# The narrow column tile of an expert moved from last to first place, in a two-layer hybrid backbone kernel on one core

## The chip, the core and the metric

The kernel runs on one core of a Trainium2 chip. The metric is the device time of one execution in microseconds (us); for the kernel before, three runs gave a median of 1191.35 us (1188.44 to 1191.83). A time is the number from the device; the span of the profiled execution, from the first instruction to the last, is a little shorter.

## The reference, cut to what matters

Two groups of 128 tokens (context tokens and latent tokens, D = 1024) go through two layers. Each layer has token mixers and then a channel mixer. The channel mixer of layer 0 is a dense SwiGLU with 2816 hidden columns, that of layer 1 a mixture of 8 SwiGLU experts with 1408 hidden columns, two of them per token:

```python
def swiglu(h, wg, wu, wd):
    return (jax.nn.silu(h @ wg) * (h @ wu)) @ wd

def moe_swiglu(h, router, wg, wu, wd):
    probs = jax.nn.softmax((h @ router).astype(jnp.float32), axis=-1)
    top_v, top_i = lax.top_k(probs, TOP_K)
    ...
    for e in range(N_EXPERTS):
        out = out + gates[..., e:e + 1] * swiglu(h, wg[e], wu[e], wd[e])
```

Around each mixer stand an adaptive modulation, a residual sum and a LayerNorm. All is in 32-bit floats.

## The kernel before

**Products.** A product with a weight is made of three passes of TensorE in the type fp32r: high part by high part, low part by high part, high part by low part (`mm3`, lines 1398 to 1400). The weights come as 32-bit floats into `raw`; ScalarE rounds them to `w_hi` (helper `hi`, line 582), VectorE takes the rest `w_lo = raw - w_hi` (helper `lo`, line 887). In two places GpSimd does the latter for one tile (`rests`, line 483).

**Tiles and units.** A weight tile is a block of at most 1024 x 512 (a column tile of a gate or up matrix) or of 4 chunks of 128 rows x 1024 (a part of a down matrix). It is worked in PARTS = 4 units of up to 1024 elements per partition. `w_hi` and `w_lo` have one buffer per unit, so unit u of the next tile can be written once TensorE is through with unit u of this one (`parts_free`). `raw` is a ring of SLOTS = 3 tiles of two halves each. SyncE fills a half when VectorE has made both rests of that half three tiles earlier (`lo_done`), in the order of its program.

**An expert.** It has 1408 hidden columns, which the constant `WIDE` (line 34) cuts into three column tiles of 512, 512 and 384. The tiles of an expert are numbered j = 0 to 8: gate and up of column tile 0, of 1, of 2 (j = 0 to 5), then three parts of the down projection (`DOWN`, line 41), of 4, 4 and 3 chunks of 128 hidden rows. `KINDS` (line 305) lists width and chunks of the nine. The hidden values h of column tile c are silu(gate) x up; they are transposed on TensorE (`transpose_h`) and split into `hT_hi` and `hT_lo`.

**Dense layer 0.** The dense mixer is run as two experts (`expert`, lines 641, 966, 1492) with both groups of tokens, so each weight unit is used twice. The first tile behind the LayerNorm is done by group (`first_block`, line 1408): four units for group 0, with the transposes of group 1's normalized values between the second and third unit, then four units for group 1. GpSimd makes the rests of this tile (line 535), and also those of the first tile of layer 1 (line 549), while VectorE works on the residual and the LayerNorm (`residual_norm`, line 925). The last tile of the second expert is done by group too (`rows_by_group`, line 1453), so that the norm of group 0 starts under the product of group 1. In `residual_norm` VectorE's order is: sum and statistics of group 0, sum of group 1, then modulation and `xT_lo` of group 0, and then the rest of group 1.

**Experts of layer 1.** One group of up to 128 gathered tokens per pass (`one_pass`, lines 671, 1085, 1540); here 8 passes. Before its fills of tile 3 of a pass, SyncE stores the result of the pass before (`y_store`, line 382) and loads the tokens of the next one (`x_load`, line 377): it waits there until ScalarE has copied out the last down part. In pass p, behind down part 0, TensorE transposes the last hidden values and the tokens of pass p + 1 (line 1537). In the last pass GpSimd gathers the stored results of all passes (line 558, four indirect transfers). At the start of the first pass GpSimd also computes x (`make_x`, lines 498 and 499) while VectorE makes gates and rests.

Of the kernel before, what the change touches and what calls it, by code (L numbers as in the profile page):

```python
# [9 lines left out]
ACT = mybir.ActivationFunctionType  # L10
# [13 lines left out]
FF = 1408  # L24
# [3 lines left out]
COL = 512  # L28
# [5 lines left out]
WIDE = (COL, COL, FF - 2 * COL)  # L34
# [3 lines left out]
SLOTS = 3  # L38
PARTS = 4
UNIT = 1024  # L40
DOWN = [(0, 4), (4, 8), (8, 11)]
# [16 lines left out]
def program(nc, a, out):  # L58
    with ExitStack() as ctx:
# [244 lines left out]
        FULL = (COL, 4)  # L304
# [22 lines left out]
        def _(sp):  # L327
# [96 lines left out]
        def _(pool):  # L424
# [77 lines left out]
            for l in range(DEPTH):  # L502
# [60 lines left out]
        def _(act):  # L563
# [45 lines left out]
            def to_next(n, q):  # L609

                hi(q, 0, (0, 1))
                ln_std(n, 0)
                ln_scale(n, 0)
                if n < 2 * DEPTH - 1:
                    hi(q, 0, (2,))
                act.wait_ge(coef_ok, n + 1)
                modulate(n, 0)
                if n < 2 * DEPTH - 1:
                    modulated_hi(n, 0)
                    hi(q, 0, (3,))  # L620
# [6 lines left out]
                if n == 2 * DEPTH - 1:  # L627
                    hi(q, 0, (2, 3))
# [12 lines left out]
            def expert(q, ec, last):  # L641

                for j in range(PER_EXPERT):
                    nq, ns, n = q + (j + 1) // SLOTS, (j + 1) % SLOTS, (KINDS + [FULL])[j + 1]
# [14 lines left out]
                    if j in (0, 2, 4):  # L659
                        n = WIDE[j // 2]  # L660
                        multiplied(act, q + j // SLOTS, j % SLOTS)
                        for g in range(G):
                            ins = nc.scalar.activation(h[:, g, j // 2 * COL:j // 2 * COL + n], bank[g][:, 0:n], ACT.Silu)
                        ins.then_inc(g_silu, 1)
# [6 lines left out]
            def one_pass(q, p, last):  # L671

                for j in range(PER_EXPERT):
                    nq, ns, n = q + (j + 1) // SLOTS, (j + 1) % SLOTS, (KINDS + [FULL])[j + 1]
# [32 lines left out]
                    if j in (0, 2, 4):  # L707
                        c, n = j // 2, WIDE[j // 2]
                        multiplied(act, q + j // SLOTS, j % SLOTS)
                        nc.scalar.activation(h[:, 0, c * COL:c * COL + n], bank[c % 2][:, 0:n], ACT.Silu).then_inc(g_silu, 1)  # L710
# [159 lines left out]
        def _(dve):  # L870
# [54 lines left out]
            def residual_norm(n, q):  # L925
# [31 lines left out]
                else:  # L957
# [3 lines left out]
                    lo(q + 1, 0, (0, 1))  # L961
# [4 lines left out]
            def expert(q, ec, last):  # L966
                for j in range(PER_EXPERT):
                    nq, ns, n = q + (j + 1) // SLOTS, (j + 1) % SLOTS, (KINDS + [FULL])[j + 1]
# [14 lines left out]
                    if j in (1, 3, 5):  # L983
# [3 lines left out]
                        for g in range(G):  # L987
                            hc = h[:, g, c * COL:c * COL + n]
# [96 lines left out]
            def one_pass(q, p, last):  # L1085

                for j in range(PER_EXPERT):
                    nq, ns, n = q + (j + 1) // SLOTS, (j + 1) % SLOTS, (KINDS + [FULL])[j + 1]
# [15 lines left out]
                    if j in (1, 3, 5):  # L1104
# [3 lines left out]
                        hc = h[:, 0, c * COL:c * COL + n]  # L1108
# [85 lines left out]
            for l in range(DEPTH):  # L1194
# [184 lines left out]
                else:  # L1379
# [5 lines left out]
                    lo(q0, 0, (2, 3))  # L1385
# [482 lines left out]
```

## Time and profile before

| | us |
|---|---|
| median of three runs | 1191.35 (1188.44 to 1191.83) |
| the profiled execution, its own time | 1191.93 |
| its span | 1190.2 |
| TensorE busy | 1144.7 (96%) |
| VectorE busy | 871.3 |
| ScalarE busy | 689.4 |
| layer 0's dense mixer, about | 304 to 494 |
| layer 1's expert passes, about | 783 to 1171 |

The profile's page names for each engine its busy time, and in groups what it did and for whom it waited. A start time counts from the start of the span. A matmul's duration in the trace is longer than the distance between two starts, since they overlap in the array; what counts for TensorE's pace is the distance of the starts. Idle time in square brackets stands before an instruction, with what ended it.

### The profile page before, as it was taken

To read this page: it belongs to the slowest core of one execution; us is meant where nothing else is said; L and a number is where in the kernel's file an instruction comes from. 1 tells how busy PE (TensorE), PEld (TensorE's weight loads), DVE (VectorE), ACT (ScalarE), POOL (GpSimd) and SP (SyncE) were. 2 spreads that over 40 slices of the span, in tenths; PEclk is the share of its full clock that TensorE was granted. 3 is DMA by queue.
4 is the path that set the end of the run, shared out by engine and by line. 5 is a ranking of instruction groups with operands and counts; after the bars stand their busy time and mean duration, and the time that the engine had idled before them with its cause. 6 is when DMAs were issued, how large, how long until landed. Compare 5 with 4: busy or idle time off the path is not lost.

```text
span 1190.2 us, 15753 instructions
## 1 busy us (share of the span) xinstructions
PE 1144.7 (96%) x5615; PEld 904.7 (76%) x5615; DVE 871.3 (73%) x1215; ACT 689.4 (58%) x993; POOL 131.2 (11%) x144
## 2 busy tenths in 40 slices
PE   5999999999899999899999999979999999999995
PEld 1666667888689889776667888758888888888873
DVE  1676657767575445677756776699999989999988
ACT  1544445644544444444445654548888888888873
POOL 5230100001270000350010000050000000000020
PEclk7999999999999999999999999989999999999998
DMA  9998986665359856459787466359999999999991
GB/s 353 360 379 310 334 294 241 212 196 194 124 182 415 282 178 198 142 159 340 258 274 276 149 225 224 116 174 386 370 389 384 388 386 387 390 383 387 390 387 68
DMA packets 167066, 335.76 MB, mean 282 GB/s; under 512 B 6704, under 2 KB 27296, under 8 KB 167008
## 3 DMA queue, kind: packets, MB, share of 16 engines
q1 hardware_dynamic: 158432, 307.25, 72.5%
q0 software_dynamic: 8544, 27.73, 7.0%
q8 instruction: 36, 0.59, 0.2%
q14 instruction: 22, 0.18, 0.0%
q10 hardware_dynamic: 32, 0.01, 0.0%
HBM read 317.63 MB, written 17.33 MB: 281 GB/s over the span
## 4 chain that ended last, share of the span: by engine, by line
PE 90%; DVE 5%; DMA 3%; ACT 1%; SPq 0%; issue 0%; DVEq 0%; ACTq 0%
PE bank L1398 26%; PE bank L1400 25%; PE bank L1399 25%; PE bank L1601 4%; DMA raw<-in_ada_w 1%; PE bank L1667 1%; DVE w_lo L887 1%; DMA raw<-in_moe_w_down 1%; DVE xT_lo L922 1%; PE bank L1685 1%; PE bank L1675 1%; PE bank L1548 1%; PE bank L1656 1%; PE bank L1480 1%; DVE x L935 1%; PE bank L1472 1%
## 5 line engine op out<-in xcount | busy, mean ns | idle before, releaser
L887 DVE TENSOR_TENSOR w_lo<-raw,w_hi 128x1024 fp32r<-128x1024 f32 (+1 forms) x496 | 583.4, 1200 | 177.2 <-ACT w_hi L582 172.9
L582 ACT ACTIVATE w_hi<-raw 128x1024 fp32r<-128x1024 f32 (+1 forms) x504 | 503.8, 1008 | 327.9 <-PE bank L1400 316.3
L1398 PE MATMUL bank<-w_hi,xT_hi 128*128 128x512 f32 (+1 forms) x1056 | 414.4, 392 | 17.3 <-DVE xT_lo L922 9.9
L1400 PE MATMUL bank<-w_lo,xT_hi 128*128 128x512 f32 (+1 forms) x1056 | 404.3, 383 | 0.0
L1399 PE MATMUL bank<-w_hi,xT_lo 128*128 128x512 f32 (+1 forms) x1056 | 403.1, 382 | 0.0
L1398 PEld LDWEIGHTS bank<-w_hi,xT_hi 128*128 128x128 f32 x1056 | 200.8, 190 | 59.3 <-DVE w_lo L887 8.9
L1400 PEld LDWEIGHTS bank<-w_lo,xT_hi 128*128 128x128 f32 x1056 | 199.5, 189 | 35.8
L1399 PEld LDWEIGHTS bank<-w_hi,xT_lo 128*128 128x128 f32 x1056 | 200.2, 190 | 31.3
L1398 PE MATMUL bank<-w_hi,hT_hi 128*128 128x512 f32 x360 | 142.0, 394 | 1.1 <-DVE w_lo L887 1.1
L1400 PE MATMUL bank<-w_lo,hT_hi 128*128 128x512 f32 x360 | 140.5, 390 | 0.0
L1399 PE MATMUL bank<-w_hi,hT_lo 128*128 128x512 f32 x360 | 140.4, 390 | 0.0
L1398 PEld LDWEIGHTS bank<-w_hi,hT_hi 128*128 128x128 f32 x360 | 67.6, 188 | 15.5 <-DVE w_lo L887 1.8
L1400 PEld LDWEIGHTS bank<-w_lo,hT_hi 128*128 128x128 f32 x360 | 67.6, 188 | 14.3
L1399 PEld LDWEIGHTS bank<-w_hi,hT_lo 128*128 128x128 f32 x360 | 67.7, 188 | 13.3
L1601 PE MATMUL bank<-raw,cond_st 128*32 128x512 f32 x384 | 55.8, 660 | 6.3 <-DMA raw<-in_ada_w 5.8
L760 ACT ACTIVATE qkT<-bank 128x256 f32<-128x256 f32 (+1 forms) x32 | 14.0, 438 | 73.6 <-PE bank L1657 41.5
L1281 DVE TENSOR_SCALAR work<-bank,rsum 128x128 f32<-128x128 f32 x32 | 11.2, 351 | 45.8 <-PE bank L1685 45.8
L558 POOL DMA_INDIRECT work<-y_rows,row_no x4 | 6.3, 1577 | 333.4 <-DMA y_rows<-work 332.5
L483 POOL TENSOR_TENSOR w_lo<-raw,w_hi 128x1024 fp32r<-128x1024 f32 x8 | 22.7, 2867 | 155.7 <-DVE nmr L899 155.7
L768 ACT ACTIVATE work<-bank,nmx 128x128 f32<-128x128 f32 (+1 forms) x64 | 26.3, 417 | 16.9 <-DVE nmx L1264 16.5
L1262 DVE TENSOR_REDUCE mx<-bank 128x1 f32<-128x128 f32 (+1 forms) x64 | 19.9, 353 | 14.7 <-PE bank L1667 13.4
L1601 PEld LDWEIGHTS bank<-raw,cond_st 128*32 128x32 f32 x384 | 8.1, 112 | 28.7 <-DMA raw<-in_ada_w 13.8
(254 smaller groups left out, 884.4 us busy)
## 6 DMA issues: line engine op xcount, KB each, us to landing
raw<-in_w_in SPq DMA_DIRECT2D x52, 1024.0 KB, 7.4
raw<-in_ada_w SPq DMA_DIRECT2D x48, 1024.0 KB, 7.6
raw<-in_moe_w_gate SPq DMA_DIRECT2D x32, 1024.0 KB, 9.4
raw<-in_moe_w_up SPq DMA_DIRECT2D x32, 1024.0 KB, 10.1
raw<-in_moe_w_down SPq DMA_DIRECT2D x32, 1024.0 KB, 10.0
raw<-in_moe_w_gate SPq DMA_DIRECT2D x16, 768.0 KB, 11.3
raw<-in_moe_w_up SPq DMA_DIRECT2D x16, 768.0 KB, 10.5
raw<-in_moe_w_down SPq DMA_DIRECT2D x16, 768.0 KB, 9.7
```

The lines of the kernel that those rows point to most:

```text
L483: pool.tensor_tensor(w_lo[:, unit, 0:n], raw[:, r, at:at + n], w_hi[:, unit, 0:n].bitcast(F32), ALU.subtract)\
L582: nc.scalar.activation(w_hi[:, unit, 0:n], raw[:, r, at:at + n], ACT.Copy).then_inc(hi_done, 1)
L760: nc.scalar.activation(qkT[:, j % 2, 0:n], bank[QK][:, 0:n], ACT.Copy).then_inc(j_qkT, 1)
L768: ins = nc.scalar.activation(e_buf[:, j % 2, i, 0:n], scores(i)[:, 0:n], ACT.Exp, bias=nmx[:, j % 2, i:i + 1], scale=SCALE, accum_out=esum ...
L887: V.tensor_tensor(w_lo[:, unit, 0:n], raw[:, r, at:at + n], w_hi[:, unit, 0:n].bitcast(F32), ALU.subtract).then_inc(lo_done, 1)
L922: V.tensor_tensor(xT_lo[:, :, g, :], modulated[:, g, :, :], xT_hi[:, :, g, :].bitcast(F32), ALU.subtract)\
L935: then(V.scalar_tensor_tensor(out=x[:, g, :], in0=x[:, g, :], scalar=ALPHA, in1=gate_bc[n % 2][g], op0=ALU.mult, op1=ALU.add))
L1262: ins = V.tensor_reduce(mx[:, y, i:i + 1], scores(i)[:, 0:n], AX_X, ALU.max)
L1398: pe.matmul(o, hi, wh, start=start, stop=False)
L1399: pe.matmul(o, lo, wh, start=False, stop=False)
L1400: return pe.matmul(o, hi, wl, start=False, stop=stop)
L1601: ins = pe.matmul(bank[ADA][32 * j:32 * j + 32, :], cond_st[:, 4 * half + j, at:at + 32], raw[:, r, c0:c0 + COL], start=v == 0 and half == ...
```

## The change

The order of an expert's column tiles becomes 384, 512, 512, and the down parts become chunks 0 to 2, 3 to 6 and 7 to 10. The place where a column tile begins is no longer a multiple of 512 and is listed in `BEGIN`. Where code assumed that an expert's first tile is full (the tile ahead of the first expert, the tile behind the last), it gets the kind of the first tile. The hidden units and the sums are the same; the sum over hidden chunks is cut in other places.

```diff
-WIDE = (COL, COL, FF - 2 * COL)
+WIDE = (FF - 2 * COL, COL, COL)
+BEGIN = (0, FF - 2 * COL, FF - COL)
...
-DOWN = [(0, 4), (4, 8), (8, 11)]
+DOWN = [(0, 3), (3, 7), (7, 11)]
...
             def expert_part(j, half, wg, wu, wd):
                 if j < 2 * CHUNKS:
-                    return columns((wg, wu)[j % 2], half, j // 2 * COL, WIDE[j // 2])
+                    return columns((wg, wu)[j % 2], half, BEGIN[j // 2], WIDE[j // 2])
                 return rows(wd, half, *DOWN[j - 2 * CHUNKS])
...
                     pool.wait_ge(nmr_ok, G + 1)
-                    rests(turn0[l] + Q_LAYER, 0)
+                    rests(turn0[l] + Q_LAYER, 0, KINDS[0])
...
             def to_next(n, q):
 
-                hi(q, 0, (0, 1))
+                kind = KINDS[0] if n % 2 else FULL
+                hi(q, 0, (0, 1), kind)
...
-                    nq, ns, n = q + (j + 1) // SLOTS, (j + 1) % SLOTS, (KINDS + [FULL])[j + 1]
+                    nq, ns, n = q + (j + 1) // SLOTS, (j + 1) % SLOTS, (KINDS + KINDS[:1])[j + 1]
...
-                    lo(q + 1, 0, (0, 1))
+                    lo(q + 1, 0, (0, 1), KINDS[0] if n % 2 == 0 else FULL)
...
-                    lo(q0, 0, (2, 3))
+                    lo(q0, 0, (2, 3), KINDS[0])
```

The remaining lines of the diff do the same in the other helpers: `kind` is passed on in the later calls of `to_next`, the line of `nq, ns, n` changes in all four loops over j, and `j // 2 * COL` or `c * COL` becomes `BEGIN[...]` where h is written.

## Rows read from the trace of the kernel before

**Rows 1.** Groups by form, whole span: count, busy us, mean ns, idle before.

```profile
L887 DVE TENSOR_TENSOR w_lo<-raw,w_hi 128x1024 fp32r<-128x1024 f32 x396 | 496.1, 1275 | 146.5 <-ACT w_hi L582 142.4
...
L887 DVE TENSOR_TENSOR w_lo<-raw,w_hi 128x768 fp32r<-128x768 f32 x80 | 75.0, 956 | 26.7 <-ACT w_hi L582 26.4
```

**Rows 2.** Timeline, TensorE, last pass, tiles 5 and 6: start us, us, what.

```profile
1151.69 0.33 PE L1399 MATMUL bank<-w_hi,xT_lo 128*128 128x384 f32 x1
...
1153.77 0.33 PE L1399 MATMUL bank<-w_hi,xT_lo 128*128 128x384 f32 x1
...
1155.07 0.40 PE L1399 MATMUL bank<-w_hi,hT_lo 128*128 128x512 f32 x1
...
1157.12 0.39 PE L1399 MATMUL bank<-w_hi,hT_lo 128*128 128x512 f32 x1
```

**Rows 3.** Chain that ended last: the token transposes of two passes in succession.

```profile
875.01 0.87 PE bank L1537 x8
...
922.31 0.87 PE bank L1537 x8
```

**Rows 4.** Window of a middle pass: us, busy by engine, clock, DMA share, GB/s.

```profile
897.00:944.00 47.00, 47.00 (x229) 40.41 (x229) 43.33 (x45) 38.80 (x47) 0.00 (x0) 1.00 1.05 387
```

**Rows 5.** Timelines of GpSimd, VectorE and TensorE, entry of the dense mixer.

```profile
294.90 11.35 POOL L483 TENSOR_TENSOR w_lo<-raw,w_hi 128x1024 fp32r<-128x1024 f32 x4 [18.99 <-DVE nmr L899]
...
295.44 2.92 DVE L935 SCALAR_TENSOR_TENSOR x<-x,work 128x1024 f32<-128x1024 f32 x1
...
300.96 3.06 DVE L922 TENSOR_TENSOR xT_lo<-work,xT_hi 128x1024 fp32r<-128x1024 f32 x1 [1.19 <-ACT xT_hi L607]
...
304.07 0.50 PE L1398 MATMUL bank<-w_hi,xT_hi 128*128 128x512 f32 x1 [3.10 <-DVE xT_lo L922]
...
308.52 1.03 PE L1472 MATMUL bank<-ident,work 128*128 128x128 f32 x8
...
313.50 0.50 PE L1398 MATMUL bank<-w_hi,xT_hi 128*128 128x512 f32 x1 [1.19 <-DVE xT_lo L922]
```

**Rows 6.** Timelines of ScalarE and VectorE, same stretch, with one uncontended twin.

```profile
289.76 1.23 DVE L935 SCALAR_TENSOR_TENSOR x<-x,work 128x1024 f32<-128x1024 f32 x1
...
306.30 1.24 ACT L593 ACTIVATE work<-x,nmr,rstd 128x1024 f32<-128x1024 f32 x1 [0.51 <-DVE nmr L899]
```

**Rows 7.** Timelines of VectorE and TensorE, from the dense mixer to layer 1.

```profile
489.81 0.69 DVE L932 TENSOR_TENSOR work<-bank,work 128x512 f32<-128x512 f32 x1 [1.28 <-PE bank L1400]
...
494.78 2.98 DVE L935 SCALAR_TENSOR_TENSOR x<-x,work 128x1024 f32<-128x1024 f32 x1
...
500.35 3.06 DVE L922 TENSOR_TENSOR xT_lo<-work,xT_hi 128x1024 fp32r<-128x1024 f32 x1 [1.19 <-ACT xT_hi L607]
...
503.68 0.77 PE L1398 MATMUL bank<-w_hi,xT_hi 128*128 128x512 f32 x1 [3.34 <-DVE xT_lo L922]
```

**Rows 8.** Timeline, VectorE, start of the first expert pass.

```profile
785.22 2.37 DVE L1029 TENSOR_SCALAR rs<-rs 128x2 f32<-128x2 f32 x1
...
790.07 11.26 DVE L887 TENSOR_TENSOR w_lo<-raw,w_hi 128x1024 fp32r<-128x1024 f32 x6
```

**Rows 9.** Timelines of SyncE and ScalarE, a middle pass: y store, tile 3's first unit.

```profile
982.41 0.37 SPq L382 DMA_DIRECT2D y_rows<-work  x1
...
992.48 1.06 ACT L582 ACTIVATE w_hi<-raw 128x1024 fp32r<-128x1024 f32 x1 [0.44 <-DMA raw<-in_moe_w_up]
```

**Rows 10.** Issue to landing: tile 4's first half, issued at 843.9 and at 1080.4.

```profile
DMA to landing us min/median/max: 11.2/11.2/11.2
...
DMA to landing us min/median/max: 11.6/11.6/11.6
```

**Rows 11.** Timeline, ScalarE, last pass: tile 4's third unit.

```profile
1145.43 1.58 ACT L582 ACTIVATE w_hi<-raw 128x768 fp32r<-128x768 f32 x2 [2.76 <-DMA raw<-in_moe_w_gate]
```

**Rows 12.** Windows of two idle places, columns as in rows 4.

```profile
504.00:508.00 4.00, 4.00 (x10) 3.12 (x10) 1.23 (x5) 1.54 (x2) 3.75 (x5) 0.50 0.40 99
780.00:784.00 4.00, 2.03 (x15) 1.71 (x14) 3.61 (x14) 0.60 (x1) 3.04 (x4) 1.00 0.55 222
```

More of the change, by code:

```diff
@@ L614, in to_next @@
                 if n < 2 * DEPTH - 1:
-                    hi(q, 0, (2,))
+                    hi(q, 0, (2,), kind)
                 act.wait_ge(coef_ok, n + 1)
@@ L619, in to_next @@
                     modulated_hi(n, 0)
-                    hi(q, 0, (3,))
+                    hi(q, 0, (3,), kind)
                 ln_std(n, 1)
@@ L627, in to_next @@
                 if n == 2 * DEPTH - 1:
-                    hi(q, 0, (2, 3))
+                    hi(q, 0, (2, 3), kind)
             def ada_copy(i):
@@ L662, in expert @@
                         for g in range(G):
-                            ins = nc.scalar.activation(h[:, g, j // 2 * COL:j // 2 * COL + n], bank[g][:, 0:n], ACT.Silu)
+                            ins = nc.scalar.activation(h[:, g, BEGIN[j // 2]:BEGIN[j // 2] + n], bank[g][:, 0:n], ACT.Silu)
                         ins.then_inc(g_silu, 1)
@@ L673, in one_pass @@
                 for j in range(PER_EXPERT):
-                    nq, ns, n = q + (j + 1) // SLOTS, (j + 1) % SLOTS, (KINDS + [FULL])[j + 1]
+                    nq, ns, n = q + (j + 1) // SLOTS, (j + 1) % SLOTS, (KINDS + KINDS[:1])[j + 1]
                     ahead = j < PER_EXPERT - 1 or not last
@@ L967, in expert @@
                 for j in range(PER_EXPERT):
-                    nq, ns, n = q + (j + 1) // SLOTS, (j + 1) % SLOTS, (KINDS + [FULL])[j + 1]
+                    nq, ns, n = q + (j + 1) // SLOTS, (j + 1) % SLOTS, (KINDS + KINDS[:1])[j + 1]
                     ahead = j < PER_EXPERT - 1 or not last
@@ L987, in expert @@
                         for g in range(G):
-                            hc = h[:, g, c * COL:c * COL + n]
+                            hc = h[:, g, BEGIN[c]:BEGIN[c] + n]
                             ins = V.tensor_tensor(hc, hc, bank[2 + g][:, 0:n], ALU.mult)
@@ L1087, in one_pass @@
                 for j in range(PER_EXPERT):
-                    nq, ns, n = q + (j + 1) // SLOTS, (j + 1) % SLOTS, (KINDS + [FULL])[j + 1]
+                    nq, ns, n = q + (j + 1) // SLOTS, (j + 1) % SLOTS, (KINDS + KINDS[:1])[j + 1]
                     ahead = j < PER_EXPERT - 1 or not last
@@ L1107, in one_pass @@
                         dve.wait_ge(g_silu, (p + DENSE_PARTS) * CHUNKS + (c + 1))
-                        hc = h[:, 0, c * COL:c * COL + n]
+                        hc = h[:, 0, BEGIN[c]:BEGIN[c] + n]
                         V.tensor_tensor(hc, hc, bank[2 + c % 2][:, 0:n], ALU.mult).then_inc(h_ok, 1)
```

2 lines of the change are left out of this document (1 added, 1 removed).

## The prediction

> **What bounds the kernel now.** I read the window of one pass in the middle of layer 1 first [rows 4]. TensorE is busy in all of its 47.00 us at a granted clock of 1.00, and the DMA engines are busy at 1.05 with 387 GB/s: two limits lie on each other. The same transposes recur after 47.30 us [rows 3], and that is TensorE's own work: 162 steps of 512 columns and 48 of 384. A step is 0.228 us at 512 (2.05 us over 9) and 0.173 at 384 (2.08 over 12) [rows 2], so 36.9 + 8.3, and some 2.1 for 19 transposes. So a pass can't become shorter by an order of tiles, only longer. In the dense mixer each weight unit is used twice and the DMA has room. What an order of tiles can change lies where TensorE waits: at the two ends of the dense mixer, at the start of the first pass, and in the last pass.
>
> **The change part by part.**
>
> *Sums.* The same columns, bytes, transposes and chunks; a full tile takes TensorE 24 x 0.228 = 5.46 us per group of tokens, a narrow one 24 x 0.173 = 4.16, a down part of 3 chunks 18 x 0.228 = 4.10 [rows 2]. Nothing is added, only moved: 0 us. The silus, products and splits of h have the same sizes in another order. Of the widths that change place, a rest of 1024 costs VectorE 1.275 us and one of 768 0.956 [rows 1]; both are hidden under TensorE inside an expert.
>
> *Entry of the dense mixer.* Four rests of GpSimd take 11.35 us, and VectorE's operations with two inputs in SBUF wait for them: the sum takes 2.92 and xT_lo 3.06 [rows 5], where the sum alone takes 1.23 [rows 6]. So the sum waited 1.7 us; with a start at 294.9 GpSimd's operation ended at about 297.1, 2.2 us for 1024 elements. By length I take 1.7 us for 768. Then GpSimd's first ends at 296.6, the sum at 297.85 (before 298.4), the second GpSimd operation at 299.5, the third at 301.2; xT_lo of group 0, which needs the modulation (ready at about 300.4), waits for the third and ends at 302.4 instead of 304.02. TensorE starts 1.6 us earlier. All of VectorE's later work moves by the same 1.6: the normalized values of group 1 are ready at 305.9 instead of 307.5 [rows 6]. TensorE's transposes of them, before at 308.52 behind two units at the slow clock [rows 5], stand behind two narrow units now and start at 305.9 to 306.3. From the transposes to TensorE's start on group 1 it was 313.50 - 308.52 = 4.98 us [rows 5], a chain of ScalarE and VectorE with no weights in it; so group 1 starts at about 311.1, 2.4 us earlier. Its block is 1.3 us shorter, but 2 x 1.3 = 2.6 us of columns must be made up in later tiles: 2.4 + 1.3 - 2.6 = 1.1 us gained. Bounds: 0, if GpSimd's and VectorE's operations meet otherwise, to 2.0. The Trainium skill, "SBUF — State Buffer", section "SBUF: two separate sides", says that VectorE with two SBUF inputs and GpSimd share one port pair by a lock held for a whole instruction; by that rule this case's gain is real for every operation caught behind a shorter one, and the trace's 2.92 against 1.23 agrees.
>
> *Exit of the dense mixer.* The last down part is done by group, and has 4 chunks now instead of 3. TensorE's end of group 1 stays, its end of group 0 comes 5.46 - 4.10 = 1.36 us earlier. VectorE was waiting for TensorE at the sum of group 0 [rows 7], so its statistics and the release of GpSimd's rests of layer 1's first tile (which stays full) come some 1.2 us earlier, at about 493.0 instead of 494.3. The sum of group 1 can't come earlier (it waits for TensorE's end at 493.9) but meets a GpSimd operation that ends at 495.2 and no longer at 496.5: it ends at 496.45 instead of 497.76. xT_lo meets the third one, and ends at 502.1 instead of 503.41; TensorE follows [rows 7]. Gain 1.2 us, bounds 0 (ScalarE, which makes two high parts first, is late) and 1.4.
>
> *Start of the first pass.* GpSimd computes x there, in four operations, and VectorE's gates and rests alternate with them: a gate operation of 2 elements takes 2.37 us, and six rests 11.26 [rows 8], where six alone would take 7.65 [rows 1]. A narrow tile ends its rests 0.6 us earlier, but the alternation is paced by GpSimd. Putting narrow rests between its operations, tile 1's last rest ends at 797.8 to 798.2 instead of about 799.0, and tile 2 starts at about 799.1 instead of 802.2; of these 3.1 us 2.6 are columns still to come. Gain 0.2 to 0.6, I take 0.4.
>
> *The passes between.* Here the question is whether weights arrive. A pass moves 17.5 half-tiles of 1 MB (16.5 of weights, 1 of y store and x load), so one is worth 47.30 / 17.5 = 2.70 us. Tile 3 is the tight one: ScalarE waits 0.44 us for it [rows 9], with nothing lost on TensorE: tile 3 starts at 3 x 5.46 + 0.5 for transposes = 16.9 us of the pass, the unit was wanted at 12.3, and less the wait, one high part and one rest (together some 2.8) there are 1.8 us of cover. Counted from the start of a pass, its first half is the 8th MB and is wanted when the first unit of tile 2 is done: 2 x 5.46 + 1.37 = 12.3 us, against 8 x 2.70 = 21.6 of supply: 9.3 behind the origin of the count. In the new order it is the 7th MB, wanted at 2 x 4.16 + 1.37 = 9.7 against 18.9: 9.2. The same. But the tiles behind it are tighter than before: tile 4 8.8 (before 8.0), tile 5 8.7 (before 7.0). SyncE's stay at the y store, 2.5 us into the pass [rows 9], ends some 0.8 us earlier, because the last down part has full units; tile 3's fill is then issued at 2.9 us for a landing at about 10. That is 7 us against the 9 of before, but still more than the 2 MB in front of it and itself need, so the queue doesn't run dry, by a margin of about 1 us. The supply falls behind a little from pass to pass (11.2 us to landing in pass 1, 11.6 in pass 6 [rows 10]), and passes start 0.4 us earlier relative to it; so the landing in pass 6 is some 0.9 us late, and of the cover (tile 3 starts at 14.1 now: 14.1 - 9.7 - 0.9 - 2.3) 1.2 us are left, or 0.9 where VectorE's product of the tile before is in the way. Cost 0. Bounds: nothing, or what the first rival says.
>
> *Last pass.* GpSimd's gathers take the DMA some 2 MB, and ScalarE waits 2.76 us for one half [rows 11]. The pass takes about 49.3 us where TensorE's work is 46.7: 2.6 us lost. In the new order the delay falls on tiles with 0.8 to 1.7 us less slack, against a start 2.5 us earlier in the pass, and all that follows has more. Placing the same delay (some 6 us less the 1.35 of the absent x load) on the new order gives 3.0 to 3.6 us lost. Cost 0.6, bounds -1 and +2.
>
> *End.* The last down part is 1.36 us longer behind its third unit, which gives ScalarE and VectorE more cover for scaling the gathered rows. Nothing is gained on TensorE: 0.
>
> *Sum.* -1.1 - 1.2 - 0.4 + 0.6 = -2.1 us. On the profiled execution's own 1191.93 us (span 1190.2 and 1.7 around it) that is 1189.8. The median of the runs is 0.6 lower, so I forecast 1189.2.
>
> **The rivals.**
>
> *The tiles behind the third stall (slower).* The place is tiles 3 to 5 of every pass. If the DMA queue runs dry once in a pass while SyncE stands at the y store, or if ScalarE's wait grows beyond its cover, TensorE loses time in every pass. It decides from the point where the landing slips by about 1 us more than now. Price: 0.5 to 1.4 us (the latter is 5.46 - 4.10, the most that a fill can be put off) in 7 passes, 3.5 to 9.8 us; with the gain of 2.1, 1190.6 to 1197, typically 1194.5. For it speak the DMA share of 1.05 and the drift [rows 4, 10], against it that the count for tile 3 comes out the same. Chance 0.13.
>
> *The clock stays up (faster).* At the exit of the dense mixer TensorE stands idle for 3.3 us, and then works at a granted clock of 0.50, its 1.2 GHz level [rows 7, 12]: twelve steps take 5.1 us instead of 2.7. Idle for 2.0 us, at 781 to 783, its clock stayed at 1.00, 2.4 GHz [rows 12]. The change brings the idle time from 3.3 to about 2.1 us. If the clock does not fall, 2.4 us more are gained at the first two units, less 0.4 for waiting on group 1's values: 2.0, and 0.4 at the entry, where the idle time falls from 3.1 to 1.5 but the chain of VectorE rules. Time: 1186.8. Against it: two idle places, one with a fall and one without, don't say where between 2.0 and 3.3 us the fall begins, nor that the length of one idle time alone decides. Chance 0.25.
>
> *Nothing gained at the ends.* If GpSimd's shorter operations meet VectorE's so that xT_lo is caught by one more of them, the gains of entry and exit are gone: 1191 to 1192. For it: the order of meeting was read off three long operations only. Chance 0.15.
>
> **How the numbers follow.** My forecast, 1189.2, has 0.47, the rivals 0.13, 0.25 and 0.15. A measurement can tell a change from none at about 0.3%, 3.6 us: faster means below 1187.8, slower above 1194.9. Faster: the case of the clock, 0.25, and 0.05 of the forecast's tail, 0.30. Slower: half of the stalling case and little else, 0.09. The same: 0.61. The range reaches from the clock's case with the upper bounds of the gains (1185.0) to the middle of the stalling case (1194.5).
>
> **What would show it.** Right: xT_lo of the dense mixer's entry ends near 302.4, TensorE's first product of layer 1 near 502 less the 1.1 us from above; the middle passes recur after 47.30 us with TensorE busy throughout; the last pass takes 49.5 to 50.5. Wrong: a period of the passes above 47.4, waits of TensorE for w_lo in passes 1 to 6, or a y store whose issue comes later in the pass than 2.5 us. A clock of 1.00 behind the exit of the dense mixer would show the second rival.

## The result, and the profile after

| | before | changed |
|---|---|---|
| median of 20 runs, us | 1191.16 (1188.2 to 1194.9) | 1193.71 (1191.3 to 1195.4) |
| ratio, with its 95% interval | | 1.0022 (1.0013 to 1.0031) |
| span of the profiled execution | 1190.2 | 1192.7 |

The changed kernel is 0.22% slower, 2.6 us. That is less than the 0.3% which the prediction counts as a difference, but 20 runs against 20 do tell it from none; the forecast was 2.1 us the other way. The ratios here and below, and the range above, leave out the slow runs, which are one of the changed kernel (1291.0 us at a granted clock of 0.84) and one of e6 (1806.3 us at 0.59). Differences between kernels in us are worked out from the ratios.

In the lines of the changed kernel the helpers stand one line lower for ScalarE, GpSimd and SyncE (L484, L583) and two for VectorE and TensorE (L889, L937, L1400).

Entry of the dense stretch, timelines of GpSimd, VectorE and TensorE; these answer to [rows 5]:

```profile
295.06 9.23 POOL L484 TENSOR_TENSOR w_lo<-raw,w_hi 128x768 fp32r<-128x768 f32 x4 [18.77 <-DVE nmr L901]
...
295.61 2.38 DVE L937 SCALAR_TENSOR_TENSOR x<-x,work 128x1024 f32<-128x1024 f32 x1
...
300.57 2.02 DVE L924 TENSOR_TENSOR xT_lo<-work,xT_hi 128x1024 fp32r<-128x1024 f32 x1 [1.19 <-ACT xT_hi L608]
...
302.65 0.45 PE L1400 MATMUL bank<-w_hi,xT_hi 128*128 128x384 f32 x1 [1.36 <-DVE xT_lo L924]
...
311.13 0.44 PE L1400 MATMUL bank<-w_hi,xT_hi 128*128 128x384 f32 x1 [1.83 <-DVE xT_lo L924]
```

The shorter operations of GpSimd let VectorE through earlier, and TensorE starts at 302.65 instead of 304.07, group 1 at 311.13 instead of 313.50. Exit of that stretch, VectorE and TensorE; these answer to [rows 7]:

```profile
494.87 1.81 DVE L937 SCALAR_TENSOR_TENSOR x<-x,work 128x1024 f32<-128x1024 f32 x1
...
499.57 2.80 DVE L924 TENSOR_TENSOR xT_lo<-work,xT_hi 128x1024 fp32r<-128x1024 f32 x1 [1.25 <-ACT xT_hi L608]
...
502.63 0.47 PE L1400 MATMUL bank<-w_hi,xT_hi 128*128 128x512 f32 x1 [2.05 <-DVE xT_lo L924]
```

At the first product of layer 1's experts the changed kernel is 2.1 us ahead (780.96 us against 783.09). All of the loss comes after that. Windows of the changed kernel (us, busy time and count by engine in the order PE, PEld, DVE, ACT, POOL, then the granted clock, the DMA share and GB/s):

```profile
312.00:316.00 4.00, 4.00 (x16) 4.00 (x15) 1.56 (x2) 1.69 (x2) 0.00 (x0) 0.57 0.00 0
504.00:508.00 4.00, 4.00 (x18) 3.32 (x17) 0.42 (x2) 1.38 (x2) 2.75 (x5) 0.66 0.68 123
784.00:808.00 24.00, 19.20 (x74) 15.73 (x73) 22.73 (x16) 14.04 (x17) 12.18 (x6) 0.79 0.79 268
832.00:840.00 8.00, 8.00 (x39) 6.92 (x38) 7.45 (x9) 6.80 (x10) 0.00 (x0) 1.00 0.93 304
897.00:944.00 47.00, 47.00 (x229) 40.41 (x228) 43.20 (x45) 38.20 (x47) 0.00 (x0) 1.00 1.05 387
1146.00:1150.00 4.00, 2.09 (x6) 1.67 (x7) 3.37 (x4) 3.29 (x4) 0.00 (x0) 0.80 1.05 386
1150.00:1154.00 4.00, 4.00 (x17) 3.19 (x17) 3.44 (x4) 2.76 (x5) 0.00 (x0) 0.77 1.06 387
```

And of the kernel before, the same four stretches of layer 1 where they differ:

```profile
784.00:808.00 24.00, 19.60 (x77) 14.84 (x76) 23.60 (x17) 14.39 (x14) 13.76 (x7) 0.86 0.77 252
832.00:840.00 8.00, 8.00 (x36) 6.50 (x36) 7.30 (x9) 7.05 (x10) 0.00 (x0) 1.00 1.05 386
1146.00:1150.00 4.00, 3.29 (x21) 2.94 (x20) 3.70 (x5) 2.96 (x5) 0.00 (x0) 1.00 1.06 381
1150.00:1154.00 4.00, 4.00 (x26) 3.96 (x24) 3.45 (x5) 3.72 (x6) 0.00 (x0) 1.00 1.05 384
```

The middle passes take as long as they did: the transposes recur after 47.33 us, in the chain that ended last:

```profile
921.17 0.87 PE bank L1539 x8
968.50 0.87 PE bank L1539 x8
```

Under this equal period one thing did change. What ScalarE waited for from 862 to 1105 us, in total us, times and longest, before:

```profile
ACT w_hi L582 <- DMA raw<-in_moe_w_up: 3.2, 6, 0.6
```

and changed:

```profile
ACT w_hi L583 <- DMA raw<-in_moe_w_up: 17.3, 20, 1.6
ACT w_hi L583 <- DMA raw<-in_moe_w_gate: 3.3, 5, 0.7
```

ScalarE has to wait for weights 20.6 us in 25 times instead of 3.2 us in 6. TensorE's period does not show it, so the cover was enough, but less of it is left. The same waits are found in e3, e7 and e11 (17.7 to 22.8 us), which share the order of the passes behind the first, and not in e2 and e8 (1.7 and 3.1 us), which do not.

**The queue's account.** This is an attempt to book the loss on the DMA queue: one adds up what the DMA engines carry from 770 us on, when the experts of layer 1 are about to begin. Windows of the kernel before, columns as above:

```profile
770.00:808.00 38.00, 30.71 (x153) 24.29 (x152) 33.13 (x66) 18.16 (x20) 16.80 (x10) 0.91 0.55 183
808.00:856.00 48.00, 48.00 (x234) 41.16 (x233) 44.20 (x46) 39.73 (x49) 0.00 (x0) 1.00 1.04 377
856.00:1158.00 302.00, 300.57 (x1460) 258.50 (x1458) 275.81 (x284) 246.69 (x293) 6.31 (x4) 1.00 1.05 387
1158.00:1180.00 22.00, 19.82 (x73) 13.38 (x73) 18.77 (x23) 12.50 (x16) 0.00 (x0) 1.00 0.24 87
```

And of the changed kernel:

```profile
770.00:808.00 38.00, 30.82 (x151) 26.08 (x151) 33.91 (x68) 19.28 (x24) 17.31 (x10) 0.87 0.62 212
808.00:856.00 48.00, 48.00 (x234) 41.25 (x233) 44.47 (x45) 39.71 (x47) 0.00 (x0) 1.00 1.02 366
856.00:1158.00 302.00, 299.47 (x1436) 256.04 (x1435) 274.21 (x281) 242.21 (x289) 5.97 (x4) 0.99 1.05 386
1158.00:1180.00 22.00, 22.00 (x87) 15.81 (x87) 17.96 (x19) 14.20 (x17) 0.00 (x0) 1.00 0.31 116
```

GB/s times us is bytes: 183 x 38 + 377 x 48 + 387 x 302 + 87 x 22 make 143.8 MB before, and 144.7 MB in the changed kernel; the GB/s are rounded. The packets of the hardware queue from 770 to 1172 us, with their MB in the middle, give the difference as 1.05 MB, first before, then changed:

```profile
q1 hardware_dynamic: 72304, 138.42, 94.0%
q1 hardware_dynamic: 72304, 139.47, 95.2%
```

The kernels use the same weights; the difference lies in what the three slots of `raw` already hold. The fills issued from 560 to 776 us, by source, with their size and time to landing, before:

```profile
raw<-in_moe_w_gate SPq DMA_DIRECT2D x4, 1024.0 KB, 5.7
raw<-in_moe_w_up SPq DMA_DIRECT2D x3, 1024.0 KB, 6.5
```

and changed:

```profile
raw<-in_moe_w_gate SPq DMA_DIRECT2D x2, 1024.0 KB, 6.1
raw<-in_moe_w_gate SPq DMA_DIRECT2D x2, 768.0 KB, 4.8
raw<-in_moe_w_up SPq DMA_DIRECT2D x2, 768.0 KB, 5.7
raw<-in_moe_w_up SPq DMA_DIRECT2D x1, 1024.0 KB, 5.0
```

Seven fills either way, but four of them are 256 KB smaller: 1.05 MB less is there when the stretch begins in which the queue hardly rests. At the 387 to 388 GB/s of that stretch 1.05 MB are 2.7 us of transport. Counting in this way (bytes / 387.5 GB/s is time of transport, the rest of the time is idle, and the bytes left at 1158 us say when the queue ends):

| kernel | MB from 770 us | idle, us | queue ends | last product starts |
|---|---|---|---|---|
| before | 143.8 | 21.7 | 1162.9 | 1170.9 |
| changed | 144.7 | 21.1 | 1164.6 | 1173.5 |
| e1, dense only | 143.8 | 18.9 | 1160.1 | 1168.0 |
| e4, second dense expert only | 143.8 | 19.0 | 1160.0 | 1168.1 |
| e2, pass 0 only | 144.7 | 21.4 | 1164.9 | 1172.4 |
| e3, later passes only | 143.9 | 23.7 | 1165.0 | 1172.8 |
| e5, pass 0 as 512, 384, 512 | 144.6 | 17.5 | 1160.6 | 1167.7 |
| e11, all but pass 0 | 143.9 | 19.5 | 1160.9 | 1168.3 |
| e6, before, make_x later | 143.8 | 19.9 | 1161.0 | 1169.0 |
| e7, changed, make_x later | 144.9 | 15.6 | 1159.4 | 1167.5 |
| e9, changed, less in last pass | 143.8 | 20.2 | 1161.4 | 1169.3 |
| e10, before, less in last pass | 142.8 | 21.8 | 1160.4 | 1168.2 |

In e8 and e12 the queue ends before 1158 us, so this count doesn't apply. TensorE's last product starts 7.1 to 8.9 us behind the counted end of the queue in all of the others, in most 7.4 to 8.1. The packets themselves end 1.0 to 1.9 us later than the count (1164.7 us before, 1165.9 changed), and the rows are of one execution of each kernel. The table books where the bytes and the idle time are; that they set the end is for the runs to show. The Trainium skill, "HBM Reference", section "Specifications (TRN2)", gives about 358 GB/s for each of two cores that stream at once and more for one that streams alone; this case's 387 GB/s, on one core, agrees with the latter.

### The profile page after: what moved, and what is told of

The parts are those of the page before. It is cut to its first block, busy times and chain, and to the rows that moved or that the text cites. A ratio compares the mean times of both kernels' runs of the same rounds, so it can differ in the third digit from the quotient of the medians.

```text
span 1192.7 us, 15760 instructions
## 1 busy us (share of the span) xinstructions
PE 1147.0 (96%) x5615; PEld 907.8 (76%) x5615; DVE 870.2 (73%) x1215; ACT 687.0 (58%) x993; POOL 129.6 (11%) x144
## 4 chain that ended last, share of the span: by engine, by line
PE 89%; DVE 5%; DMA 3%; ACT 2%; SPq 0%; issue 0%; DVEq 0%; ACTq 0%
PE bank L1400 26%; PE bank L1402 25%; PE bank L1401 25%; PE bank L1603 4%; DVE w_lo L889 1%; DMA raw<-in_ada_w 1%; DMA raw<-in_moe_w_gate 1%; PE bank L1669 1%; PE bank L1687 1%; DVE xT_lo L924 1%; PE bank L1677 1%; PE bank L1550 1%; PE bank L1482 1%; PE bank L1474 1%; PE bank L1658 1%; ACT work L601 1%
## 5 line engine op out<-in xcount | busy, mean ns | idle before, releaser
L889 DVE TENSOR_TENSOR w_lo<-raw,w_hi 128x1024 fp32r<-128x1024 f32 (+1 forms) x496 | 586.1, 1206 | 180.0 <-ACT w_hi L583 175.4
L583 ACT ACTIVATE w_hi<-raw 128x1024 fp32r<-128x1024 f32 (+1 forms) x504 | 500.9, 1008 | 334.5 <-PE bank L1402 303.1
L1400 PE MATMUL bank<-w_hi,xT_hi 128*128 128x512 f32 (+1 forms) x1056 | 415.8, 394 | 17.2 <-DVE w_lo L889 7.7
L1400 PEld LDWEIGHTS bank<-w_hi,xT_hi 128*128 128x128 f32 x1056 | 201.6, 191 | 58.4 <-DVE w_lo L889 11.7
L1400 PE MATMUL bank<-w_hi,hT_hi 128*128 128x512 f32 x360 | 141.8, 394 | 0.0
L1400 PEld LDWEIGHTS bank<-w_hi,hT_hi 128*128 128x128 f32 x360 | 67.6, 188 | 13.9 <-issue 0.4
L484 POOL TENSOR_TENSOR w_lo<-raw,w_hi 128x768 fp32r<-128x768 f32 (+1 forms) x8 | 20.6, 2615 | 159.3 <-DVE nmr L901 159.3
L1264 DVE TENSOR_REDUCE mx<-bank 128x1 f32<-128x128 f32 (+1 forms) x64 | 19.9, 353 | 14.7 <-PE bank L1669 13.4
```

The lines of the kernel that those rows point to most:

```text
L484: pool.tensor_tensor(w_lo[:, unit, 0:n], raw[:, r, at:at + n], w_hi[:, unit, 0:n].bitcast(F32), ALU.subtract)\
L583: nc.scalar.activation(w_hi[:, unit, 0:n], raw[:, r, at:at + n], ACT.Copy).then_inc(hi_done, 1)
L889: V.tensor_tensor(w_lo[:, unit, 0:n], raw[:, r, at:at + n], w_hi[:, unit, 0:n].bitcast(F32), ALU.subtract).then_inc(lo_done, 1)
L1264: ins = V.tensor_reduce(mx[:, y, i:i + 1], scores(i)[:, 0:n], AX_X, ALU.max)
L1400: pe.matmul(o, hi, wh, start=start, stop=False)
```

## The experiments

All kernels with the order of tiles changed in part are built with one table in place of the constants (e1 to e4 with a table of true and false, to the same effect):

```diff
-WIDE = (COL, COL, FF - 2 * COL)
+NARROW = (0, 0, 2, 2)
+WIDES = [[FF - 2 * COL if c == at else COL for c in range(3)] for at in NARROW]
+BEGINS = [(0, w[0], w[0] + w[1]) for w in WIDES]
-DOWN = [(0, 4), (4, 8), (8, 11)]
+DOWNS = [[(b // P, (b + n) // P) for b, n in zip(begins, widths)] for begins, widths in zip(BEGINS, WIDES)]
```

`NARROW` has the place of the narrow tile in the first dense expert, the second, pass 0, and the passes behind it (there are eight passes, 0 to 7; where an expectation says 1 to 8 it means all behind pass 0). (2, 2, 2, 2) is the kernel before, (0, 0, 0, 0) the changed one.

My theory at first was that the gain is made at the exit of the dense stretch and lost to the new order in the first and the last pass, in the first because GpSimd's `make_x` meets all four rests of a narrow tile 1 (below this part is the lock theory).

**e1 (0, 0, 2, 2), e2 (2, 2, 0, 2), e3 (2, 2, 2, 0), e4 (2, 0, 2, 2).**

> Both dense experts in the order 384, 512, 512; all passes of layer 1 in the old order. My theory (the gain is at the end of the dense stretch, and is lost again in the first and in the last pass because of the new order there): the first narrow tile of layer 1 is gone, so the start of the first pass is as before and the 2.1 us by which the changed kernel was ahead at 780 us reach the end: 1188.8 to 1189.5 us where the kernel before takes 1191.2, ratio 0.998. Rival A (the passes are bound by what the queue has brought, so whatever is gained ahead of them is waited away again): the ratio stays within 0.9990 and 1.0010, and PE waits more in the first passes. Rival B (the loss comes with the dense stretch, as a different meeting of clock and passes): as slow as the full change, ratio 1.002.

Measured: 1187.27 us against 1191.77, ratio 0.9970 (0.9959 to 0.9981), 3.6 us faster. That is more than expected. The gain of the dense stretch reaches the end in full (TensorE's first product of layer 1's experts starts at 780.79 us, 2.3 us earlier than before); rivals A and B fall.

> Only pass 0 of layer 1 in the new order; dense experts and passes 1 to 8 old. My theory: pass 0 alone costs what the full change lost in its first pass, 2.0 to 2.5 us: GpSimd's make_x meets all four rests of the narrow tile 1, and the half clock stays longer; 1193.3 to 1193.8 us, ratio 1.0018 to 1.0021. Rival (the first pass lost time only because the change came 2 us ahead of the gather and the queue there): no loss from the order, ratio 0.9990 to 1.0005.

Measured: 1192.91, ratio 1.0011 (1.0001 to 1.0020): 1.3 us. There is a loss, smaller than expected. This kernel owes the same 1.05 MB more as the changed one, and the interval (0.1 to 2.4 us) does not reach the 2.7 us that they take.

> Passes 1 to 8 in the new order, pass 0 and the dense experts old. My theory: the middle passes keep their 47.3 us, the last one takes 51.5 to 52 us in place of 49.3, since more product work stands behind tile 4's second half and the clock falls after the wait: 1193.3 to 1193.9 us, ratio 1.002. Rival (the last pass is late in the full change only because the first passes left the queue shallower): the last pass takes at most 0.6 us more, ratio 1.0000 to 1.0006.

Measured: 1193.05, ratio 1.0011 (0.9997 to 1.0025). The period is 47.4, and the last pass is longer than before by 0.9 us in the trace, not by 2.3: the loss of the last pass in the changed kernel isn't all its own. What this kernel shows besides is a queue that runs dry where pass 1 begins:

```profile
832.00:836.00 4.00, 4.00 (x19) 3.34 (x18) 4.00 (x6) 3.12 (x5) 0.00 (x0) 1.00 0.81 239
```

> Only the second dense expert in the new order (its last down part is then 4 chunks and its successor layer 1 is old). My theory: the whole dense gain is at the exit, so this alone gives as much as both dense experts: residual L887/L889's chain starts earlier against GpSimd, the wait of PE there is 2.0 us in place of 3.3 and the half clock is shorter: 1188.8 to 1189.7 us. Rival (the gain at the exit is the clock's place, set by what happened at the entry, and goes when the entry is old): less than 0.8 us, above 1190.4 us.

Measured: 1189.64, ratio 0.9978 (0.9970 to 0.9987), 2.6 us. The exit carries most of the dense gain, as expected.

Added up, e1, e2 and e3 would make the changed kernel 1.0 us faster than before, and it is 2.6 slower. It was this, and the account of bytes above, that made me put a new theory beside the first: supply. From 808 us on the queue has hardly a gap, so by this theory the end is set by what it still owes and by its idle time so far.

**e5 (2, 2, 1, 2): one narrow tile ahead instead of two.**

> Only pass 0 changed: its columns in the order 512, 384, 512 (down parts of 4, 3 and 4 chunks); everything else as before. Supply theory (new, from the traces of the first four runs: from 808 us on the queue carries 388 GB/s without a gap, so the end is set by how much it still has to carry at that point, and the three slots hold 1.05 MB less when the first two tiles of pass 0 are narrow, worth 1.05 MB / 388 GB/s = 2.7 us): here one tile of the three held ahead is narrow, 0.52 MB less, so the queue's end moves by +1.35 us; ratio 1.0005 to 1.0015. Lock theory (the loss of the first pass comes from narrow tile 1 whose four rests all meet GpSimd's make_x): tiles 0 and 1 are wide here, no loss, ratio 0.9995 to 1.0003.

Measured: 1191.41 against 1190.50, ratio 1.0006 (0.9996 to 1.0017). This is in the range that the expectation gives for supply, but the interval holds the other theory's values too: no verdict. The bytes carried from 770 us on are 144.6 MB, more than before. The expectation counted two narrow fills, 0.52 MB, but the seventh of those filled ahead, the first half of tile 3, is narrow too: 0.79 MB, which at 387.5 GB/s are 2.0 us and not 1.35, the very end of the interval. Its profiled execution had no fall of the clock at the exit of the dense stretch, though that stretch has the instructions of the kernel before (granted clock 1.00 from 500 to 512 us, before 0.72), and was 3 us ahead at the first product of layer 1's experts (780.12 us); so its row in the table has little idle time.

**e6 and e7: make_x out of the first pass**, in the kernel before and in the changed one:

```diff
                 for g in range(G):
                     pool.wait_ge(xhat_ok, G * n + g + 1)
+                    pool.wait_ge(h_ok, (DENSE_PARTS + 2 + 2 * g) * CHUNKS + 3)
                     then(pool.tensor_tensor(x[:, g, :], xhat[:, g, :], ln_gb[n][:, 0, :], ALU.mult))
+                    pool.wait_ge(h_ok, (DENSE_PARTS + 3 + 2 * g) * CHUNKS + 3)
                     then(pool.tensor_tensor(x[:, g, :], x[:, g, :], ln_gb[n][:, 1, :], ALU.add))
```

> The kernel before, with GpSimd's four long operations of the last make_x moved out of the first pass, one each behind tile 5 of passes 2, 3, 4 and 5. Supply theory: the waits of 2.55, 1.48 and 0.38 us at tile 1 and the half clock from 792.4 to 799.3 us go, the fills are asked for earlier and the 7 us that the queue stands idle between 784 and 804 us shrink; the gain reaches the end: 3 to 6 us, 1185.5 to 1188.5, ratio 0.995 to 0.9975. Rival (the moved operations hold VectorE up as long in the middle passes, where PE has no slack): within 1 us of the kernel before.

Measured: 1188.59, ratio 0.9975 (0.9963 to 0.9987), 3.0 us faster.

> The changed kernel with the same move of make_x. Lock theory: the 2.3 us that the new order loses in the first pass were the meeting with make_x, so they go and this stands at least 0.5 us below e6 thanks to the dense exit: ratio to e6 0.9985 or less. Supply theory: the 1.05 MB that the slots hold less are still owed, and the 1.6 us in which the queue runs dry at 832 to 840 us too: this stands 1 to 3 us above e6 in spite of the dense gain: ratio to e6 1.001 to 1.0025.

Measured: 1190.55, ratio 1.0001 (0.9990 to 1.0012); against e6 1.0026, 3.1 us, and 2.0 us by the two medians. So the order costs time although the meeting with `make_x` is out of the first pass, dense gain included, which is what supply expected and the lock theory didn't.

The traces show that this is no clean test. From the first product of layer 1's experts to the transposes of the next tokens the new order took 1.0 us more than the old one with `make_x` there (45.6 and 44.6 us), and takes 2.1 us less with `make_x` gone (36.8 in e7, 38.9 in e6, of which 1.7 us are e6's half clock). So the meeting was a real part of the first pass's loss, as the lock theory says. TensorE of e7 is 6.4 us ahead of e6 at these transposes (815.43 against 821.84 us) and then gives 3.4 us back in the middle passes, where five periods take 242.6 us, in e6 239.1 us and undisturbed some 236.6 us. e8, with the old order in these passes, is nearly as far ahead (816.44 us) and takes 239.2 us, so it is not the lead that costs the 3.4 us. There ScalarE waits for weights for 22.1 us in e7 and 3.7 us in e6 (862 to 1105 us), and the moved operations stand in the same passes. So the new order and the moved operations together cost more there than the operations do in the old order. How much of it comes from late weights is not told apart, and without these 3.4 us e7 would not stand above e6. The two profiled executions even end the other way round than the ratio has it (spans 1186.7 and 1188.2 us). e7 settles neither theory.

**e8 (0, 0, 2, 2) with make_x later.**

> Dense experts in the new order, all passes in the old one, and make_x moved as in e6. Supply theory: both gains are gains in how early the queue is kept full and add up: 2.5 to 3.5 us below e6, 1183 to 1185.5, ratio to before 0.992 to 0.995. Rival (the two gains share one wait): no better than the better one of e1 and e6.

Measured: 1185.70, ratio 0.9964 (0.9950 to 0.9979). Less than the expected 0.992 to 0.995, and not apart from e1 (0.9970) and e6 (0.9975): the rival, that the two gains share one wait, is not excluded. Part of the lead is given back: TensorE waits 0.3 us in each of the four passes into which an operation was moved (47.72 of 48 us busy), and in the last pass 2.71 us at once for a late half, with a half clock behind it:

```profile
940.00:988.00 48.00, 47.72 (x231) 40.67 (x230) 45.75 (x45) 39.36 (x48) 3.24 (x1) 1.00 1.05 384
1140.00:1150.00 10.00, 10.00 (x51) 9.79 (x50) 8.90 (x11) 7.96 (x11) 0.00 (x0) 0.83 1.05 385
```

**e9 and e10: 1.05 MB less in the last pass**, in the changed kernel and in the one before:

```diff
+                        src, k, n = expert_part(o, j, half, *w)
+                        if less and j == 3:
+                            src, k = src[:, 0:2, :], 2
-                        fill(s, half, *expert_part(o, j, half, *w))
+                        fill(s, half, src, k, n)
```

> The changed kernel, but the fill of tile 3 of the last pass brings only half of its rows (2 of 4 chunks in each half, 1.05 MB less of 2.1; the other rows of the slot are old weights, so the last pass computes something else with the same instructions). Supply theory (the end follows the queue, through the waits of the last pass): the queue's end comes 2.7 us earlier, the 2.5 us that PE waits at tile 4 and the half clock behind them (1.7 us) go: 1189.5 to 1191.5, ratio 0.998 to 1.0. Rival (the last pass is long because of what its order leaves on PE and DVE, whatever the queue does): stays at 1.0015 to 1.003.

Measured: 1189.56 against 1190.51, ratio 0.9993 (0.9980 to 1.0006). That is 3.5 us less than the changed kernel's 1.0022, and the rival (the last pass is long by its order, whatever the queue does) falls. TensorE's waits of the last pass and its half clock are gone (window of e9, to be put beside the same one of the changed kernel above):

```profile
1146.00:1150.00 4.00, 4.00 (x22) 3.28 (x21) 3.04 (x3) 3.32 (x4) 0.00 (x0) 1.00 1.05 386
```

> The same 1.05 MB left out in the kernel before (tile 3 of the last pass, the other rows are old weights). Supply theory: PE waits 1.8 us in the last pass there and no clock falls, so at most 1.8 us come back: 1.0 to 1.8, ratio 0.9985 to 0.9992; the changed kernel with the same cut is then 0.5 to 1.5 us nearer to this one than without. Rival: ratio 0.9995 to 1.0005.

Measured: 1189.63, ratio 0.9988 (0.9978 to 0.9998), 1.4 us less than before, though no instruction of an engine was taken away. With 1.05 MB less in both, changed and before differ by 0.05% (give or take 0.16%) and no longer by 0.22%. The last pass waits for the queue in both kernels, and in the changed one for longer. That shows where the time is lost, in the last pass behind the queue; it does not show that the 1.05 MB of the first tiles are what makes the queue late.

**e11 (0, 0, 2, 0): the full change, pass 0 put back.**

> The full change with pass 0 alone put back to the old order. Supply theory: the slots hold their 1.05 MB again, the queue ends 2.7 us before that of the changed kernel, and the last pass waits less; what is left of passes 1 to 8 costs the 1.6 us of dry queue at 832 to 840: 1189.5 to 1191, ratio 0.9985 to 0.9998. Rival (the losses are the last pass's own and the clock's): above 1192.5, ratio 1.001 or more.

Measured: 1190.17, ratio 0.9999 (0.9987 to 1.0010), 2.7 us less than the changed kernel: what 1.05 MB take at 388 GB/s, but also about what TensorE loses in the first pass of the changed kernel (2.3 us, below). Both theories ask for a gain here, so the run prices the order of pass 0 and does not choose between them. The bytes from 770 us on are back at 143.9 MB. Against e1, which differs in the passes behind pass 0 alone, it is 0.9999 to 0.9970, 3.5 us slower. Part of this is the dry queue where pass 1 begins (371 GB/s from 808 to 856 us against e1's 381, 1.2 us), and 1.1 us more are seen in the last pass (from its transposes of tokens to the last product 61.4 us, less 1.36 for the longer last part, against 59.0). The two traces don't show the whole difference: the last products start at 1168.3 and 1168.0 us, and e11's execution had no fall of the clock at the entry of the dense stretch.

**e12 (0, 0, 2, 2), make_x in halves, spread over more passes:**

```diff
+            for i in range(8):
+                g, step, half = i // 4, i // 2 % 2, i % 2 * COL
+                pool.wait_ge(xhat_ok, G * 3 + g + 1)
+                pool.wait_ge(h_ok, (DENSE_PARTS + 1) * CHUNKS + 2 + 2 * i)
+                then(pool.tensor_tensor(x[:, g, half:half + COL], (x if step else xhat)[:, g, half:half + COL],
+                                        ln_gb[3][:, step, half:half + COL], ALU.add if step else ALU.mult))
```

> Dense experts in the new order, passes in the old one, and the last make_x in eight halves of 128x512, spread over passes 1 to 6 (behind every second h_ok from tile 3 of pass 1 on). In e8 the four whole operations cost 0.6 us of pass each (48.0 us in place of 47.3 in passes 3 to 6). If a half holds the port pair for half as long and VectorE's lead over PE covers it, the passes stay at 47.3 us and this is 1 to 2.5 us below e8: 1183.5 to 1184.8, ratio 0.993 to 0.9955. If the hold costs what it lasts whatever its size: as e8, 0.9965.

Measured: 1184.94, ratio 0.9951 (0.9936 to 0.9966), 5.8 us faster than the kernel before and the best of the versions here. TensorE is busy in all of the middle passes, which it wasn't in e8, and its wait of 2.30 us in the last pass has no half clock behind it:

```profile
940.00:988.00 48.00, 48.00 (x232) 41.02 (x231) 44.87 (x45) 39.56 (x47) 3.71 (x2) 1.00 1.05 386
1140.00:1150.00 10.00, 8.26 (x46) 7.70 (x47) 8.95 (x10) 7.62 (x11) 0.00 (x0) 1.00 1.05 383
```

Against e8 the intervals overlap (0.9951 and 0.9964) and the two spans are alike (1183.6 and 1183.4), so that halves are better than whole operations is not shown.

## Why the prediction was wrong

**The terms that failed most** are two, by TensorE's rows: the start of the first pass, forecast as a gain of 0.4 us and measured as a loss of 2.3, and the last pass, forecast as a loss of 0.6 and measured as one of 2.3. Against the lead of 2.1 us from the dense mixer they make, to 0.1 us, the 2.6 us by which the last product starts later. The period of the middle passes and both chains of the dense mixer came as forecast; the entry gained 1.0 us less than forecast, which goes with the new place of the clock's fall, and the exit 0.8 us more.

**A term put at nothing without a full reason** is the first: "The same columns, bytes, transposes and chunks ... Nothing is added, only moved: 0 us". Over the whole kernel the bytes are the same, but not over the stretch in which the queue is a limit: there they are 1.05 MB more. The prediction had read both numbers it needed, the 387 GB/s at a share of 1.05 and the three slots that are filled ahead, and called the passes limited by two things at once; but it then counted only the order in which tiles arrive within a pass. That the bytes are there is shown. That they cost the 2.7 us which they take in transport is argued: e11 gives 2.7 us for pass 0 with all that its order does, e2 alone only 1.3.

**The first rival's times** don't follow from its price. It asks for 3.5 to 9.8 us, and on 1189.2 us that is 1192.7 to 1199.0, not "1190.6 to 1197". The upper end of the range comes from this rival. The measured 1193.71 us lies below that end, but not because the rival came true: its place was the middle passes, and they did not stall. That the number is in the range is luck.

**"The queue doesn't run dry, by a margin of about 1 us"** failed too. It held for the middle passes, whose period of 47.33 us and full TensorE are as forecast. But it ran dry at the turn from pass 0 to pass 1: 304 GB/s from 832 to 840 us, where the kernel before has 386, 8 x 82 / 387 = 1.7 us. TensorE does not wait there (it is busy for all 8.00 us), and so nothing near it shows a cost; by the account it comes due in the last pass. In the middle passes ScalarE's cover held, as forecast, though its waits for weights rose from 3.2 to 20.6 us, the longest 1.6 us.

**Dense entry**, forecast -1.1, measured -0.1. The chain was right to 0.1 us: TensorE on group 1 at 311.13 for "about 311.1". What failed is that the fall of the clock was taken as tied to the place: it left 304 to 308 us (1.00 there now), and came at 312 to 316 (0.57) instead. In other kernels with the same dense stretch it came there or near it too (e1, e8, e9, e12), or not at all (e7 and e11, 1.00 from 300 to 316 us).

**Dense exit**, forecast -1.2. TensorE's start came 1.05 us earlier, or 1.3 when the 0.2 us by which the whole stretch was later are taken off, so the term was right; it was the clock that gave more: 0.66 and 1.00 in the windows from 504 and from 508 us, before 0.50 [rows 12] and 0.83. At 781 us the lead was 2.1. That is a part of the rival "the clock stays up", and e4, which has this chain and this clock alone, is 2.6 us faster at the end. Clock and order do not go together in every execution, though: from 500 to 512 us the granted clock was 0.72 in the kernel before, e2, e3 and e10, but 0.86 in e6 and 1.00 in e5, which have the same dense stretch; with the new one it was 0.86 in seven kernels and 1.00 in e8.

**First pass**, forecast -0.4, measured +2.3 by TensorE: the transposes of the next tokens stand 1.15 us earlier than before, but 1.36 us of down part are still behind them instead of ahead, and the pass began 2.1 us earlier. By rows it is 0.4 us more of waits (4.8 and 4.4) and a clock of 0.79 instead of 0.86 over 24 us, 1.7 us. The prediction had this stretch paced by GpSimd alone and has no term for the clock in it. With `make_x` moved, e7 has one wait of 0.79 us there and no half clock (1.00 from 784 to 808 us). Whether this loss is what reaches the end, or the bytes are, stays open: e7 still stands above e6, but with 3.4 us lost on the way that may be its own, and up to 808 us the queue of the changed kernel was idle for less time than before, not more (212 GB/s from 770 to 808 us against 183).

**Last pass**, forecast +0.6 with a bound of +2, measured +2.3 (from the last transposes of tokens to the last product 63.0 us, less the 1.36, against 59.4). ScalarE waits for the half that is late in both kernels; this is the changed one's row to [rows 11]:

```profile
1145.54 2.00 ACT L583 ACTIVATE w_hi<-raw 128x1024 fp32r<-128x1024 f32 x2 [3.05 <-DMA raw<-in_moe_w_gate]
```

ScalarE starts on it at 1145.5 us, in the kernel before at 1145.4, in spite of the lead of 2.1 us at 781: by the account the lead has been spent on the bytes owed and the dry queue. The forecast had put the same delay on the new order; it did not carry a debt of the queue from pass to pass, nor the fall of the clock (0.80 and 0.77 from 1146 to 1154 us, about 1.7 us) which came behind the longer wait of TensorE, 2.04 us.

**What stays open.** Shown is that the changed kernel loses in the last pass, behind the queue (e9, e10), that pass 0's order is worth 2.7 us of it on top of the rest (e11), and that the queue has 1.05 MB more to carry. Not shown is which of these makes pass 0 cost what it does: the bytes, or the waits and the half clock of its first tiles. No run adds or takes away bytes at the first tiles alone. The parts alone (e2 and e3, 1.3 us each) cost less than on top of the dense gain (2.7 by the changed kernel against e11, 3.5 by e11 against e1). Each difference has an uncertainty of 1.2 to 1.9 us, so they may be the same; that the clock falls in the last pass of the changed kernel and not in e3 would be one cause, seen in one execution of each only. Executions of one kernel differ by about as much as the effects here: those of the kernel before with a mean granted clock of 0.989 or more took 1190.0 us, the others 1191.9 us (medians of 11 and 21, measured beside e1). The changed kernel took 1192.2 and 1193.9 us in the two kinds, some 2 us more in either, so its loss is not a matter of their mixture.

## What to carry to other kernels

Where a long stretch runs with a queue that hardly rests, an order of tiles can change the bytes already on chip when the stretch begins, and the queue's idle time: add up the bytes from the start of the stretch to its end in both versions, and ask where the end of the queue lies. In this kernel the small tile did best at the front of the dense mixer and behind the front of the passes (e1, e12). Look also at the waits that have cover: they don't show in the period, but tell what is left for the next disturbance. And look at the place of a fall of the clock after every change of a wait, since it can move to another wait rather than go.

## What the runs showed of the hardware

**The clock.** Behind single waits of TensorE for a late half in the last pass, all between 1.7 and 2.8 us, it fell in the changed kernel (2.04 us, 0.80), in e6 (2.15), in e8 (2.71) and in e7 (1.79), and did not fall in e12 (2.30), whose row stands above, nor in e11 (1.78). e6, then e7:

```profile
1140.00:1150.00 10.00, 7.85 (x36) 7.24 (x35) 5.95 (x7) 4.76 (x7) 0.00 (x0) 0.83 1.05 384
1140.00:1150.00 10.00, 10.00 (x40) 8.07 (x40) 8.17 (x9) 7.76 (x9) 0.00 (x0) 0.84 1.05 388
```

In e3 the same idle time, split into waits of at most 1.3 us, leaves it at 2.4 GHz, with TensorE busy for 5.4 of 8 us:

```profile
1142.00:1146.00 4.00, 2.71 (x13) 1.91 (x11) 2.36 (x2) 2.00 (x2) 0.00 (x0) 1.00 1.04 394
1146.00:1150.00 4.00, 2.73 (x12) 1.96 (x11) 2.47 (x3) 2.85 (x3) 0.00 (x0) 1.00 1.05 386
```

So the length of a wait alone does not say whether a fall follows, and a fall is worth about as much as the wait (1.7 us each time). The Trainium skill, "TensorE: Matmul & The Clock Gate", section "HAM oscillation — how this bites in real kernels", describes how waiting for a transfer brings the clock down to 1.2 GHz and so costs more than the wait; the rows of the changed kernel and of e6 agree, those of e12 and e3 show that it need not follow.

**GpSimd beside VectorE.** A GpSimd operation on 128x1024 with two inputs in SBUF, put in a middle pass where VectorE is busy for some 44 of 47 us, made the pass 0.6 us longer (47.3 to 47.9, e6); one or two of 128x512 in a pass made it 0.0 to 0.4 us longer (47.3 to 47.7, e12). In e7, with the new order in these passes, the passes behind the four operations took 48.5 to 49.5 us.
